# Moving the streamed operands of a two-block transformer kernel to other SBUF addresses

## The reference

```python
# first block
xn = rms_norm(h, norm1_g)
proj = xn @ w_in                                   # 1024 -> all branches
for n, y in enumerate((y_a, y_b, y_c, y_d)):
    merged += sigmoid(xn @ w_gate[n] + b_gate[n]) * (y @ w_branch[n])
h = h + merged @ w_out
h = h + square(relu(rms_norm(h, norm2_g) @ w_ff1)) @ w_ff2
h = h + sigmoid(rms_norm(h, norm3_g) @ w_ple_gate + b_ple_gate) * (p @ w_ple)
x = rms_norm(h, final_g)
# second block
z = modulate(rms_norm(x, norm1_g_2), sh1, sc1) @ w_in_2 + b_in_2
merged = sigmoid(ga) * (ym @ p_mlstm_2) + sigmoid(gb) * (ya @ p_moba_2)
x = x + g1 * (merged @ w_out_2)
hh = modulate(rms_norm(x, norm2_g_2), sh2, sc2)
x = x + g2 * ((silu(hh @ w_gate_2) * (hh @ w_up_2)) @ w_down_2)
return rms_norm(x, normf_g_2)
```

## The kernel before

| tiles | start | modulo 512 |
|---|---|---|
| whi, wlo | 36992, 53376 | 128 |
| Ahi, Alo | 85664, 93856 | 160 |
| Yhi, Ylo (three each) | 150656 and on | 128 |
| Fhi, Flo | 111712, 144480 | 96 |
| Bhi, Blo | 177248, 199776 | 96 |
| Mhi, Mlo | 111712, 119904 | 96 |
| Ymhi, Ymlo, Yahi, Yalo | 184992 and on | 160 |
| Uhi, Ulo | 111680, 134208 | 64 |
| hib, lob (rows of 1032 bytes) | 111712, 119968 | 96, 160, then 8 more per row |
| hi0, lo0 (rows of 1032 bytes) | 205472, 213728 | 160, 224, then 8 more per row |
| aq, ak; a8 | 195712, 199808; 156128 | 128; 480 |

## Time and profile before

### The profile page before, as it was taken

One profiled execution on the slowest core, in us unless ns is written; L12 is line 12 of the kernel. 1 busy time (PEld: TensorE's weight loads), 2 busy tenths in 40 slices (PEclk: granted clock), 3 DMA queues, 4 the chain that ended last, 5 costly groups with the idle time before them and its releaser, 6 DMA issues.

```text
span 934.4 us, 18432 instructions
## 1 busy us (share of the span) xinstructions
PE 909.6 (97%) x7356; PEld 882.3 (94%) x7356; DVE 729.5 (78%) x1146; ACT 565.8 (61%) x819; POOL 1.9 (0%) x9
## 2 busy tenths in 40 slices
PE   7999999999999999999999999999999999999995
PEld 6999989999999999999999988998989999999995
DVE  6778989979887899898865988968779885555554
ACT  7848356775576676664446778557685664444452
POOL 0000000000000000000000000000000000000000
PEclk9999999999999999999999999999999999999998
DMA  9756535556765689998855566443536556666541
GB/s 317 250 184 219 162 125 176 159 180 214 260 234 172 227 297 338 342 320 298 318 182 176 158 192 184 164 150 114 158 114 199 184 174 188 186 192 190 185 151 46
DMA packets 52533, 188.78 MB, mean 202 GB/s; under 512 B 5968, under 2 KB 6240, under 8 KB 52320
## 3 DMA queue, kind: packets, MB, share of 16 engines
q1 hardware_dynamic: 52304, 187.60, 60.8%
q10 hardware_dynamic: 144, 0.00, 0.0%
HBM read 186.53 MB, written 1.05 MB: 201 GB/s over the span
## 4 chain that ended last, share of the span: by engine, by line
PE 80%; DVE 12%; ACT 6%; issue 2%; DMA 0%; DVEq 0%; ACTq 0%
PE bank L989 23%; PE bank L992 23%; PE bank L991 23%; DVE wlo L1022 3%; ACT whi L1815 2%; PE bank L963 1%; PE bank L965 1%; PE bank L964 1%; DVE cv L1096 1%; DVE hsc L1500 1%; DVE scr L1195 1%; PE bank L694 1%; DVE Alo L1057 1%; ACT P L1926 1%; PE bank L939 1%
## 5 line engine op out<-in xcount | busy, mean ns | idle before, releaser
L1022 DVE TENSOR_TENSOR wlo<-raw,whi 128x1024 fp32r<-128x1024 f32 x297 | 361.0, 1221 | 128.5 <-ACT whi L1815 128.1
L1815 ACT ACTIVATE whi<-raw 128x1024 fp32r<-128x1024 f32 x297 | 312.0, 1056 | 214.2 <-PE bank L992 198.1
L989 PE MATMUL bank<-Alo,whi 128*128 128x256 f32 x1376 | 390.7, 284 | 2.5 <-ACT Ahi L1835 1.4
L992 PE MATMUL bank<-Ahi,whi 128*128 128x256 f32 x1376 | 384.6, 280 | 0.0
L991 PE MATMUL bank<-Ahi,wlo 128*128 128x256 f32 x1376 | 384.5, 279 | 0.0
L989 PEld LDWEIGHTS bank<-Alo,whi 128*128 128x128 f32 x1376 | 259.3, 188 | 7.3 <-issue 4.2
L991 PEld LDWEIGHTS bank<-Ahi,wlo 128*128 128x128 f32 x1376 | 259.4, 189 | 0.6 <-issue 0.2
L992 PEld LDWEIGHTS bank<-Ahi,whi 128*128 128x128 f32 x1376 | 259.2, 188 | 0.0
L991 PE MATMUL bank<-Fhi,wlo 128*128 128x256 f32 (+1 forms) x288 | 81.0, 281 | 0.0
L992 PE MATMUL bank<-Fhi,whi 128*128 128x256 f32 (+1 forms) x288 | 80.9, 281 | 0.0
L989 PE MATMUL bank<-Flo,whi 128*128 128x256 f32 x256 | 72.2, 282 | 0.0
(11 more groups left out here) (391 smaller groups left out, 1356.8 us busy)
## 6 DMA issues: line engine op xcount, KB each, us to landing
raw<-in_stream SPq DMA_DIRECT2D x297, 512.0 KB, 4.1
araw<-in_ada SPq DMA_DIRECT2D x48, 512.0 KB, 5.5
TB<-in_TB SPq DMA_DIRECT2D x1, 1536.0 KB, 7.1
H<-in_xT SPq DMA_DIRECT2D x4, 256.0 KB, 5.4
out<-H SPq DMA_DIRECT2D x4, 256.0 KB, 2.2
bc<-in_bc SPq DMA_DIRECT2D x1, 896.0 KB, 5.4
raw<-in_stream SPq DMA_DIRECT2D x2, 256.0 KB, 4.3
mats<-in_mats SPq DMA_DIRECT2D x1, 449.0 KB, 8.5
```

The lines of the kernel that those rows point to most:

```text
L989: pe.matmul(os[j], wh, xl, start=k == 0 and (wide or j == 0), stop=False, skip_group_check=not wide)
L992: i = pe.matmul(os[j], wh, xh, start=False, stop=k == K - 1 if wide else last, skip_group_check=not wide)
L1022: v.tensor_tensor(wlo[:, s % NHL, :], raw[:, s % NRAW, :], whi[:, s % NHL, :].bitcast(F32), ALU.subtract).then_inc(*lo_v.up(s))
L1815: a.activation(whi[:, s % NHL, :], raw[:, s % NRAW, :], ACT.Copy).then_inc(*hi.up(s))
```

## The change

Only allocations change. One gap of 64 bytes is put ahead of `Ahi`, and the small tensors `mod`, `modg`, `shb`, `spare` go in front of it. The gaps at the head of the four regions are removed, since the persistent part now ends at a residue of 64. The shifted operands get rows of 384 elements (1536 bytes), of which 258 are used: `hib`, `lob` as a view of `Fhi`, and `hi0`, `lo0` as a view of a new tensor `shifted` that lies over `Yahi` and what comes behind it instead of behind `hsc`. `mv` and `mo` move in front of `gap3`, over the end of `lob`; `bc2`, `mpad` and the others of the mixer come behind it. No instruction, wait or loop changes.

By the same adding up, A, Y, F, B, M, Ym, Ya, U and each row of the shifted operands then begin at 64 modulo 512. `whi` and `wlo` stay at 128, `raw`, `ones` and `H` where they were. `t512`, `nrm` go from 0 to 64, `aq`, `ak`, `av` from 128 to 64, `mqk` from 320 to 224, `a8`, `av2`, `Wt`, `Wp` from 480 to 384.

```diff
@@
         H = sb("H", [128, KD, T])
-        Ahi = sb("Ahi", [128, KD, T], F32R)
-        Alo = sb("Alo", [128, KD, T], F32R)
         mod = sb("mod", [128, 48])
         modg = sb("modg", [128, 24])
         shb = sb("shb", [128, 8])
         spare = sb("spare", [128, 1])[:, :]
+
+        sb("gap0", [128, 16])
+        Ahi = sb("Ahi", [128, KD, T], F32R)
+        Alo = sb("Alo", [128, KD, T], F32R)
@@
-        s1("gap1", [128, 32])
@@
-        s2("gap2", [128, 24])
@@
-        xb_ = Fhi[:, :, :].rearrange("p a t -> p (a t)")[:, 0:16 * (T + 2)].rearrange("p (h k t) -> p h k t", h=2, k=8)
-        hib, lob = xb_[:, 0], xb_[:, 1]
+        xb_ = Fhi[:, :, :].rearrange("p a t -> p (a t)")[:, 0:24 * T].rearrange("p (h k t) -> p h k t", h=2, k=8)
+        hib, lob = xb_[:, 0, :, 0:T + 2], xb_[:, 1, :, 0:T + 2]
@@
-        s3("gap3", [128, 24])
         Mhi, Mlo = s3("Mhi", [128, 8, T], F32R), s3("Mlo", [128, 8, T], F32R)
-        s3("gap", [128, 32])
+
+        mv = s3("mv", [128, 2, 512])
+        mo = s3("mo", [128, 4, T])
+        s3("gap3", [128, 144])
         bc2 = s3("bc2", [128, 512])
         mpad = s3("mpad", [128, 8, 3 + T])
         mqk = s3("mqk", [128, 8, T])
-        mv = s3("mv", [128, 2, 512])
-        mo = s3("mo", [128, 4, T])
@@
+        p3h = ExitStack()
+        shifted = sb("shifted", [128, 2, 8, 384], F32R, p3h)
+        hi0, lo0 = shifted[:, 0, :, 0:T + 2], shifted[:, 1, :, 0:T + 2]
+        p3h.close()
@@
-        hi0, lo0 = s3("hi0", [128, 8, T + 2], F32R), s3("lo0", [128, 8, T + 2], F32R)
@@
-        sb("gap4", [128, 16], F32, p4)
```

## The result

The changed kernel took 926.27 us in the median (924.24 to 932.54, 9 executions). The kernel before, in the same comparison, took 936.32 us (934.3 to 938.65). The ratio is 0.9917, with a 95% interval of 0.9889 to 0.9946: faster by 0.8%. The forecast was 913.6 us and its range 909.4 to 921, so the sign was right and the gain was less than half of what was forecast. It fell into none of the bands that the prediction gave to a cause: the first rival ended at 923, the second stood at 935. The nine executions form two groups, five from 924.24 to 926.27 and four from 931.31 to 932.54. The profiled execution took 926.27 us for a span of 925.0; the span of before was 934.4, so 9.4 us went where 21.4 were expected.

A forecast was written before the change was run, and what follows sets the result against it. The prediction took TensorE's pitch, the interval between product starts, as the bound. Its terms summed to 24.5 us, less 3.1 us lost to waits: 21.4 us, giving 914.3 us for the profiled execution, 913.6 beside the median; range 909.4 to 921.

The forecast's parts named there:

- the first rival: Turnarounds between TensorE and its helpers eat 8.6 us of the gain, leaving 15.9 us: 919.1 us; chance 0.15.
- the second: Rival: address means nothing, the tile U is quick because of its stage; time stays 935 us; chance 0.05.
- residue modulo 512: Claim that a streamed tile's start address modulo 512 sorts the pitch: 64 gives 113.3 ns, 128 gives 119.8.
- the rule quoted: Columns over 2.4 GHz plus about 2.5 ns, 109.2 ns for 256 columns, no address term: the sum would be 0.
- a second level 1.1 ns up: One stretch of Ahi and Alo ran at 117.8 ns; the new layout was assumed to have this as often.
- A, 4128 products: Ahi and Alo moved from residue 160 to 64: pitch from 116.7 to 113.3 ns, 14.0 us.
- F, 768: Feed-forward tile moved from residue 96 to 64: 4.9 ns less for each of 768 products, 3.8 us.
- Y, 576: Tile Y moved from residue 128 to 64: 6.5 ns less for each of 576 products, 3.7 us.
- shifted, 192: Shifted operands hib, lob, hi0, lo0 in rows of 1536 bytes: 120 to 114.2 ns, 1.1 us, bounds 0 and 1.5.
- the T kind: Products with streaming weights and stationary activation, 144 with A and about 96 with Y: taken as 0, bounds -0.9 and +1.5.
- given back by waits: Where VectorE's chain ends last, a faster TensorE only waits: 3.1 us of the gain lost.
- the third rival: Residue 64 is in truth like 128, so A goes from 116.7 to 119.8 ns: 949.8 us; chance 0.04.

The follow-up runs named there:

- m_x: TensorE's products alone, weights at 128, streamed tile moved through 16 residues: 113.3 to 113.9 or 117.9 ns at 64, 119.4 to 120.0 at 128.
- m_w: TensorE's products alone, streamed tile kept at 64, weights moved through 16 residues: 119.7 ns with weights at 64, 113.3 and 117.8 at 128.
- all64: The changed kernel with weights and tiles all moved on by 64 bytes, distance kept: 924.85 us, 0.9876 of the kernel before.
- diff0: The changed kernel with what lies behind the weights moved by 64 bytes, so tiles and weights both at 128: 949.82 us, 1.0134 of the kernel before.
- fill4: The changed kernel plus five full-precision products of 4 columns, each one group behind a feed-forward interruption: 926.12 us (0.9889); the same program again 921.36 us (0.9862).
- a_only: The kernel before with only Ahi and Alo moved to 64, all other tiles where they were: 930.77 us, ratio 0.9917.
- m_r: TensorE's products alone, tile at 64, weights at 128, 14 kinds of interruption six times each: stretches mostly at about 113.4 or 117.8 ns.
- m_h: m_x for six residues, meant to have ScalarE and VectorE busy beside it, but they began after TensorE was done: at 64 113.3 to 113.9 or 117.9 ns.
- m_f: TensorE's products alone, tile at 64, weights at 128, with a second small product one group behind the interruption in some kinds: 113.3 to 113.8 or 117.8 ns.
- m_s: TensorE's products alone, tile at 64, weights at 128, the interruption's own operands moved through residues: 113.3 to 113.9 or 117.8 ns, some residues mixed.
- fillx: fill4 with four further products of 4 columns, one ahead of the feed-forward, three early in the last long stretch: 935.11 us, ratio 0.9982.
- again2: The changed kernel unaltered, run once more on the chip of fill4: 926.78 us, ratio 0.9894.

## Why the prediction was right and wrong

**The bound.** TensorE's pitch sets the time: right. Its busy time fell by 12.8 us and the span by 9.4, and nearly all of the difference is the 3.3 us of longer waits. About 1.4 us of the fall is the clock at 113 to 117 us, so the change itself is worth nearer 8 us between these two profiles.

**Address as the cause.** Right, and now shown with the stream alone (m_x, m_w) and in the whole kernel (all64, diff0). The rule "residue modulo 512" was too narrow: it is the distance between weights and streamed tile modulo 256 (m_w, all64). It fitted because the weights were always at 128. Of the rule quoted from the Trainium skill, TensorE: Matmul & The Clock Gate, section "Wait — 56ns, not 53.3ns?", the runs show that its 109.2 ns were reached in no stretch; the least of all kernels was 113.3, and the same product went up to 120 by its addresses, for which it has no term.

**The term that failed.** "It has the same addresses, so a second level 1.1 ns up exists, and I assume the new layout has it as often." The level exists, but it is not 1.1 ns up at every distance. At the old distance of A the two are 116.7 and 117.9; at the new one 113.3 and 117.8. The slow level hardly depends on the move; the quick one falls by 3.4. Nor was it as often as assumed. In the stretches that hold A alone 428 of 2556 products were on the slow level in the profile of the kernel before, and 1248 of 2569 in that of the changed one; of all products some 40% were on it there. How often it comes with the old addresses is known from this one profile alone. The sum in the prediction is therefore right as the gain of a product that is on the quick level, and was applied to all. By terms, from the starts in both profiles:

| term | forecast us | measured ns, before and after | measured us |
|---|---|---|---|
| A, 4128 products | 14.0 | 116.9, 114.9 | 8.0 |
| F, 768 | 3.8 | 118.3, 117.8 | 0.4 |
| Y, 576 | 3.7 | 119.8, 115.3 | 2.6 |
| M, 192 | 1.0 | 118.4, 113.95 | 0.9 |
| Ym and Ya, B, 240 | 0.9 | 117.0, 116.6 and 118.5, 117.7 | 0.1 |
| shifted, 192 | 1.1 | 119.7, 120.9 | -0.2 |
| the T kind | 0 | A 233.2, 229.0; Y 227.4, 229.1 | 0.4 |
| the clock at 113 to 117 us | not in it | 14 products 213 apart, none | 1.4 |
| given back by waits | -3.1 | | -3.3 |
| sum | 21.4 | | 10.3 |

The span fell by 9.4; the 0.9 us between are in restarts and in the other products and are not placed.

F was lost whole: its stretches were on the slow level in all four profiles of the changed kernel. In fill4's they were not, and F gained 4.9 ns as forecast (86 starts from 460.4 to 489.3 us: 28.9 / 255 = 113.3). So the term was right for its address and wrong for its level.

The one warning in the prediction, "half of A at 1.1 ns more is 2.3 us", named the right risk at a quarter of its price: half of A at 4.4 ns is 9.1 us, and the price of all that was on it was 11.3. Subtracted from the measured 926.3 it gives 915.0, beside the forecast of 914.3 for such an execution; the clock's 1.4 us help this agreement.

**U as the pattern for all.** The prediction took one uninterrupted run as the value of an address. It said of the third rival that residue 64 had been seen with one tile in one stage, and asked only whether the stage made U quick. The stage did matter, by where its stretch began: a_only has U at 117.6 with nothing of U changed. The row of the first stretch of A at 117.8 was the visible sign of a level that belongs to the stretch and not to the tile.

**The shifted operands.** Forecast 114.2 ns, measured 120.5 to 120.9 in both stretches in all four profiles, slightly worse than the walk through the residues of the earlier trace rows. Their tiles have the right distance, but diff0, at distance 0, has them at 120.4, so their pitch doesn't follow the distance; why is open. Worth 1.3 us.

**The T kind.** Taken as 0 with bounds -0.9 and +1.5; A gained 4.2 ns per product and Y lost 1.7, together 0.4 us. Inside the bounds.

**Waits given back.** Forecast 3.1 us, found 3.3 (2.8 without the first weights), at the places named (L798, L671, L991, once L796, L669, L989). But they arose under a smaller gain than assumed, so the share given back was larger than priced. With all products quick it might have been more; no run shows it. The first rival, turnarounds, is not what happened: 3.3 us and not 8.6.

**The third rival** was placed wrong: what it feared of residue 64 holds for distance 0, which is what 128 against 128 is. Its 949.8 us are by luck exactly what diff0 took.

**Helpers.** VectorE's durations unchanged, 483 and 480 ns against 482 and 478, its idle time before L1024 7.3 us smaller than that before L1022 in the kernel before (128.5), where the rule was "about the gain", 9.4: right.

What stays open: what picks the level where the program and the addresses are the same and only the execution differs. With TensorE alone the interruption, its operands' addresses and what ran before it have a part, and within m_r the outcome mostly repeats; in the kernel 18 of 56 stretches vary. Small differences in when the helpers release TensorE might do it, or their load, but no run isolates either, since m_h had no load beside the stream.

## What to carry to other kernels

Before moving tiles for TensorE's sake, measure the pitch from starts, stretch by stretch between interruptions, in several executions: a tile's value is a pair of levels and how often each holds, and a forecast needs both. Place streamed tiles by their distance from the weights modulo 256 bytes, 64 behind them here, and not at distance 0, which loses about as much as the good distance gains. Leave a long quick stretch uninterrupted.

## What the runs showed of the hardware

- The pitch of a 128x256 product with a weight switch each time depends on the distance between weights and streamed operand modulo 256 bytes: 119.4 to 120 ns at distance 0, 113.3 or 117.8 with the tile 64 bytes behind, 116.7 or 117.9 at 32 ahead, at a granted clock of 1.00 and with all other engines idle.
- The level is taken on at the restart behind an interruption and kept until the next one: 1438 products long in the last stretch, through the change from one tile to another.
- In m_r one full-precision product of 256 columns left the stream slow six times of six, two left it quick six times of six, four slow again. It is no fixed rule: in m_f one left it quick once of four, and the addresses of the interrupting operands change the outcome too (m_s).
- A full-precision product of 4 columns took 0.14 us of the stream, and behind the last of them in fillx 1267 products ran 4.4 ns slower each.
- The changed kernel lay between 922.88 and 932.54 us in all its executions, fill4 between 919.05 and 929.71, fillx between 928.17 and 936.16, all with the tiles at the good distance; distance 0 took 949.82.
- Behind 32 products of 64x64 that took 3.4 to 3.8 us the granted clock fell in some executions of one program and not in others: 0.62 from 110 to 119 us in again2, 1.00 in the three other profiles of the changed kernel. Products of 256 columns were then 213 ns apart instead of 117.
